# The exponential of a retrieval head's scores, taken by GpSimd as a power of e instead of by ScalarE

## The reference

```
q = (hb @ w_peer_q).reshape(PEER_BLOCK, PEER_HEADS, 2, PEER_HALF)
s = einsum('thpc,hpkc->thpk', q, sub_keys)          # 2 x 128 scores per head
s1, i1 = top_k(s[:, :, 0], 16); s2, i2 = top_k(s[:, :, 1], 16)
cand = s1[..., :, None] + s2[..., None, :]           # 256 candidates
top_s, top_c = top_k(cand, 16)
idx = e1 * 128 + e2                                  # from i1, i2, top_c
g = softmax(top_s)                                   # over the 16
a = einsum('td,tkd->tk', hb, expert_u[idx])
out = einsum('tk,tkd->td', g * gelu(a), expert_v[idx])
```

## Time and profile before

| | before |
|---|---|
| median of 3 runs | 2178.06 us |
| profiled execution, time | 2179.98 us |
| profiled execution, span | 2178.1 us |
| busy: PE, DVE, ACT, POOL | 1620.5, 1409.0, 846.7, 799.1 us |
| moved by DMA | 745.14 MB, mean 342 GB/s |
| gathers of expert rows (line 1113) | 544, median 11.5 us from issue to landing |

### The profile page before, as it was taken

The page is one execution under the profiler, slowest core; times in us unless marked ns, Lnnn a source line. Parts: engine busy times, 40 slices in busy tenths (PEclk is TensorE's granted clock), DMA queues, the critical chain, the costliest instruction groups (busy, mean ns, idle before and its releaser), DMA issues.

```text
span 2178.1 us, 33399 instructions
## 1 busy us (share of the span) xinstructions
PE 1620.5 (74%) x11692; PEld 743.6 (34%) x11692; DVE 1409.0 (65%) x3339; ACT 846.7 (39%) x2418; POOL 799.1 (37%) x713
## 2 busy tenths in 40 slices
PE   7989999898998987778788989986544445444343
PEld 3555655354444443434443433332100001100000
DVE  2577766124558687877777666446776776776774
ACT  2122333102554434545456652334333333333332
POOL 1254200001323254443443333334455555455553
PEclk9999999999999998988899999998655555655555
DMA  5333466837999898899999999999999999999998
GB/s 189 143 114 114 171 213 239 308 136 266 390 417 368 343 374 359 334 383 362 372 373 408 381 391 407 399 407 398 421 421 418 421 410 407 415 418 416 421 411 347
DMA packets 125794, 745.14 MB, mean 342 GB/s; under 512 B 15892, under 2 KB 39052, under 8 KB 47916
## 3 DMA queue, kind: packets, MB, share of 16 engines
q0 software_dynamic: 78336, 570.46, 64.7%
q1 hardware_dynamic: 47292, 172.55, 21.2%
HBM read 727.36 MB, written 16.44 MB: 342 GB/s over the span
## 4 chain that ended last, share of the span: by engine, by line
PE 35%; DMA 29%; DVE 22%; issue 7%; ACT 5%; POOL 2%; SPq 0%; DVEq 0%; ACTq 0%; POOLq 0%
DMA ring<-in_expert_uv,pick 27%; PE z L1181 20%; DVE ring L1961 8%; PE acc L1353 4%; PE z L1187 2%; PE o L1216 1%; POOL ring L1113 1%; PE s L1206 1%; DVE ti L1844 1%; DVE ti L1847 1%; DVE tmp L2032 1%; DVE nm L2058 1%; PE t L1407 1%; ACT fold L1526 1%; PE o L1269 1%
## 5 line engine op out<-in xcount | busy, mean ns | idle before, releaser
L1113 POOL DMA_INDIRECT ring<-in_expert_uv,pick x544 | 667.8, 1227 | 866.4 <-PE acc L1353 792.9
L1961 DVE CUSTOM_DVE_ANT_0 ring<-ring,rep 128x1024 f32<-128x1024 f32 x544 | 664.4, 1226 | 371.4 <-DMA ring<-in_expert_uv,pick 337.1
L1353 PE MATMUL acc<-ring,fold 128*32 128x256 f32 x4352 | 454.4, 509 | 410.0 <-ACT fold L1526 409.2
L1181 PE MATMUL z<-wts,hT 128*128 128x384 f32 (+1 forms) x1408 | 607.2, 569 | 5.2 <-ACT hT L1572 2.6
L1523 ACT ACTIVATE gel<-dots 128x1 f32<-128x1 f32 x544 | 109.6, 201 | 763.0 <-DVE dots L1961 762.3
L1353 PEld LDWEIGHTS acc<-ring,fold 128*32 128x32 f32 x4352 | 107.4, 125 | 726.7 <-ACT fold L1526 650.8
L1181 PEld LDWEIGHTS z<-wts,hT 128*128 128x128 f32 x1408 | 260.0, 199 | 256.3 <-issue 191.6
L1181 PE MATMUL z<-wts,yT 128*128 128x512 f32 x384 | 189.0, 628 | 11.9 <-ACT yT L1722 7.6
L1526 ACT ACTIVATE fold<-by_pick,gel 128x32 f32<-128x32 f32 x544 | 174.8, 321 | 18.0
L1519 ACT ACTIVATE by_pick<-cst,pick 128x32 f32<-128x32 f32 x544 | 167.2, 307 | 0.0
L1836 DVE SCALAR_TENSOR_TENSOR yT<-uT,vec,yT 128x256 f32<-128x256 f32 x240 | 107.8, 500 | 2.3
(11 more groups left out here) (256 smaller groups left out, 1686.7 us busy)
## 6 DMA issues: line engine op xcount, KB each, us to landing
wts<-in_w_qkv SPq DMA_DIRECT2D x24, 1536.0 KB, 7.7
wts<-in_w_glu SPq DMA_DIRECT2D x8, 2048.0 KB, 12.2
wts<-in_w_gate SPq DMA_DIRECT2D x8, 2048.0 KB, 12.4
wts<-in_w_wq SPq DMA_DIRECT2D x8, 2048.0 KB, 11.1
ring<-in_k_cache SPq DMA_DIRECT2D x16, 768.0 KB, 7.3
ring<-in_v_cache SPq DMA_DIRECT2D x16, 768.0 KB, 8.0
ring<-in_expert_uv,pick POOLq DMA_INDIRECT x544, 11.5
wts<-in_w_cp SPq DMA_DIRECT2D x4, 2048.0 KB, 11.1
```

Of the source, the lines that this page charges most:

```text
L1113: eng.indirect_dma_start(ring[:, i % RING, :], None, a["expert_uv"], bass.IndirectOffsetOnAxis(picks(i, 0).bitcast(U32), 0)).then_inc(row_ ...
L1181: mm = eng.matmul(bank[:, 0:w], of[:, k, :], rows[:, k, :], start=(k == 0), stop=(k == depth - 1))
L1353: mm = eng.matmul(acc[b][SUB * c:SUB * (c + 1), col:col + 256], fold[:, i % 4, :], ring[:, i % RING, D + 256 * c:D + 256 * (c + 1)], start ...
L1961: eng.tensor_tensor_reduce(u, u, rep[:, j, :], 1.0, 0.0, ALU.mult, ALU.add, dots[:, i % 4:i % 4 + 1]).then_inc(dot_ready, 1)
```

## The change

`head_exp` moves from ScalarE to GpSimd. There it adds `nmx` to `cv` and raises e to the result, from a constant tile `base_e` of 16 columns. It comes right behind the gather of step at+8 (part 3 of a head belongs to step at+3, and the code looks up `PARTS` at i - 5); item 0 is done at the start of tick START - 1. The row sum, which ScalarE gave along with the exponential, is now an instruction of VectorE in `experts`, behind the wait for `ex_ready` and ahead of the reciprocal.

```diff
+        base_e = sb("base_e", [P, TOPK])
...
 (GpSimd)
+            def head_exp(q):
+                eng.wait_ge(top_ready, q + 1)
+                link(eng.tensor_scalar(ex[:, :], cv[:, :], nmx[:, :], None, ALU.add))
+                eng.tensor_tensor(ex[:, :], base_e[:, :], ex[:, :], ALU.pow).then_inc(ex_ready, 1)
...
                     eng.indirect_dma_start(ring[:, i % RING, :], None, a["expert_uv"], ...).then_inc(row_in[i % RING], 16)
+                    for q, p in PARTS.get(i - 5, ()):
+                        if p == 3:
+                            head_exp(q)
...
+            link(eng.memset(base_e[:, :], float(np.e)))
...
             for n, tick in enumerate(TICKS):
+                if n == START - 1:
+                    head_exp(0)
                 if n >= START:
                     steps_upto(MARK[n - 1] + RING)
...
 (ScalarE)
-            def head_exp(q):
-                m = P
-                eng.wait_ge(top_ready, q + 1)
-                eng.activation(ex[0:m, :], cv[0:m, :], ACT.Exp, bias=nmx[0:m, :], accum_out=exs[0:m, 0:1]).then_inc(ex_ready, 1)
...
-                    for q, p in PARTS.get(i, ()):
-                        if p == 4:
-                            head_exp(q)
...
-                if n == START - 3:
-                    head_exp(0)
...
 (VectorE, experts)
                 eng.wait_ge(ex_ready, q + 1)
+                link(eng.tensor_reduce(exs[0:m, 0:1], ex[0:m, :], AX, ALU.add))
                 link(eng.reciprocal(exs[0:m, 1:2], exs[0:m, 0:1]))
```

## The result

The changed kernel takes 2188.34 us, the median of 8 runs (2186.22 to 2191.14), beside 2178.2 us before. The ratio is 1.0045, 95% interval 1.003 to 1.006: slower by 10 us. The forecast was 2180 us and no measurable difference, the range 2166 to 2198. What happened is by its mechanism the first rival, the gathers' queue running short (2194 us, chance 0.28), at a smaller price than it named. Of all executions reported in this document only two lie far off the rest, 2793.58 and 3858.56 us, both of e10_no_exponential, and its ratio leaves them out.

The account below looks back on a forecast made before the run. Expert-row transfers were taken to set the pace after 1492 us, a mixed chain before. Terms -4 (ScalarE), +1 and +5 (GpSimd, earlier and later stretch), 0 (VectorE) sum to +2 us on 2178.06: 2180 us, range 2166 to 2198.

Parts of the forecast that it names:

- the first rival: Later stretch: in each of 16 heads the late gather meets a nearly empty queue; 1.0 x 16, 2194 us, chance 0.28.
- ScalarE's part: Exponentials and table loads leaving ScalarE: 4 us off before 1492 us; 0 after, at most 1.0 us per head regained.
- The power's length, the addition's wait and the new gap: GpSimd, later stretch: power 2.9 us, addition held until the dot's end, gap near 7 us between gather issues.
- So it fits by 0.7 us, and at+10 by about as much.: Later stretch: the first delayed gather still lands 0.7 us before its dot, the next with about that margin.
- The size: Later-stretch cost of GpSimd's late gathers: 0.3 us per head, 5 us on; bounds 16 off to 16 on.
- a power of twice the length: GpSimd, later stretch: at twice 2.9 us the row would be 2.2 us late each time, 35 us in all.
- The earlier stretch on GpSimd: Before 1492 us: the same gather lateness but less gather time on the chain; 1 us on, bounds 0 and 17.
- The decision point of the rival: Later stretch: the queue runs short from a power of 3.6 us, or a short-queue landing over 6.2 us.
- Its sum at 0: VectorE's new sum of 16 columns: 0.2 us each, hidden by later row waits, worth 0; uncovered 7 us.
- The wait at the reciprocal: VectorE waiting for GpSimd's power: it ends 3 us early in later heads; first head 0, at most 1 us.
- The rule of the Trainium skill: GpSimd and VectorE locking shared ports: a dot waits for the power's end; as a rival 2190 us, chance 0.05.
- Marks that I named: Right: later heads 40.7 to 41.0 us apart, DMA share 0.99. Wrong: the 1492 us mark moving over 5 us.

Follow-up runs that it names:

- e10_no_exponential: Changed kernel without GpSimd's addition and power: no engine takes an exponential, the tile is set to one once and VectorE sums it; 2170.0 us.
- e1: Kernel before, ScalarE keeping the exponential but losing its row sum, which VectorE takes as its own instruction; 2177.0 us.
- e5: Changed kernel with the power left out: GpSimd's addition alone writes the tile and releases VectorE; 2174.0 us.
- e6_power_twice: Changed kernel with GpSimd's power taken twice, the first into a spare tile; 2256.0 us.
- e8_two_later: Changed kernel with GpSimd's exponential placed two gathers later than the change has it; 2209.2 us.
- e9_split_place: Changed kernel with GpSimd's exponential at the change's place in the earlier stretch and one gather later for the 16 later-stretch heads; 2174.3 us.

## Why the prediction was right in its range and wrong in its largest term

By medians, the path from before to after is: VectorE's sum -1 (e1; not distinguishable from 0), ScalarE's exponentials gone -7 (e10 against e1), the addition and its waits +4 (e5 against e10), the power +14 (changed against e5). Together +10. The single terms carry some 3 to 4 us of uncertainty each. The power's +14 and ScalarE's -7 are clear of it, the addition's +4 is not. The forecast was -4 + 1 + 5 + 0 = +2: slower by less than can be told from nothing.

- **ScalarE's part.** Forecast -4 in the earlier stretch and 0 in the later; measured -7 in all, of which 3.2 in the later by the spacing, leaving about 4. The 0 was too low: the spacing could give back up to 1.0 us a head by the forecast's own bound, and it gave 0.2.
- **The power's length, the addition's wait and the new gap.** Forecast 2.9 us, until the dot's end, and "a gap near 7 us"; measured 2.97 and 7.06. Right.
- **"So it fits by 0.7 us, and at+10 by about as much."** This is the step that failed, in its second half. At+9 fits in the head shown (it waits 0.23 us; two of the 16 heads wait over 1 us). At+10 does not: it was issued at 1952.84 and its dot began at 1961.54, 8.7 us later. The prediction gave it the same margin as at+9, that is, a row one pace of 2.48 us behind that of at+9. The two dots stand 4.06 us apart here and 3.27 on average, where they stood 2.55 apart before. The step checked whether one row would land in time. What counts is whether the DMA ever has nothing to move, and it has: between 8.0 and some 10 us behind the issue of at+8 it runs thin, as the rows of at+9 begin to flow only at 8.75. Why VectorE meets that hole at the second row and not the first is not settled.
- **The size.** I put 0.3 us per later head on it, net of nothing regained, and 5 us in all. Net of ScalarE's gain the spacing rose by 0.67, 10.7 us; the power alone takes 0.85 a head. The bound of 1.0 held it. By the estimated knee of 6.2 us a power of some 2.1 us would have cost nothing. The prediction's own figure for a power of twice the length, 35 us in all, was low as well: e6_power_twice is 77 us over the kernel before, 58 of them in the later stretch (44.32 - 40.70 = 3.62 a head, where the figure has 2.2).
- **The earlier stretch on GpSimd.** Forecast +1. Of the power's +14 and the addition's +4 the spacings place 13.6 and 1.1 in the later stretch, which leaves some 4 for the earlier one, not clear of the noise.
- **The decision point of the rival** was a power of 3.6 us or a landing over 6.2 us from a short queue. The second was about met at at+9 (6.0 us from issue to dot in the head shown, 6.3 on average) and clearly at at+10 (8.2 on average). Such a margin of 0.7 us, against a landing taken from the least of one window, deserved the larger chance. That the time still came out inside the range is owed to its width: it reached past this rival.
- **VectorE.** Its sum at 0: right, e1_sum_only. The wait at the reciprocal: 4.8 us in 2 heads, within the 1 us and its bound. The power did not hold VectorE back: the dot of at+5 starts at 1949.98, 1.66 us into the power, and it stands 3.19 us behind its predecessor where it was 3.16. In all 16 later heads it starts 0.5 to 1.3 us ahead of the power's end. The rule of the Trainium skill, "SBUF — State Buffer" (SBUF: two separate sides), in which the instruction that comes second waits for the whole of the first, would have had it wait. The trace does not agree with that half of the rule.
- **Marks that I named:** the heads stand 41.37 us apart, outside the 40.7 to 41.0 that I named for being right, so this sign told of the failure; the DMA share of the later stretch (1.00) did not. The 1492 us mark was of no use, since identical programs differ there by over 6 us.

## What to carry to other kernels

Where an engine issues the transfers that set the pace, work put on it has a free allowance, the backlog in the queue. Beyond it, the work cost its full length at each occurrence here (slope 0.97 between gaps of 7.06 and 10.09 us). Measure the allowance as a gap between issues: from an issue to the moment at which the DMA would run dry, less the time from an issue to its first rows (8.0 - 1.7 us here). Whether the next row lands in time is not the test. Here the same 2.97 us of work cost 14 us behind one gather and next to nothing behind the next, because there it did not first have to wait 2.3 us for its input and for a dot.

A wait has two ends: one place later filled the queue and starved the consumer in the other stage. Choose the place by stage: e9_split_place did, and was 4 us faster than the one place that suits the later stretch.

## What the runs showed of the hardware

- GpSimd's power of 16 columns takes 2.93 to 2.94 us when nothing holds it up; with 0.56 for 1 column and 1.35 for 6 it is a straight line, 0.16 us a column.
- GpSimd's addition of 16 columns lasts 0.34 us alone, 0.62 beside two-input VectorE work and 1.37 beside a dot. A power that starts before the dot does is hardly lengthened (2.93 to 3.06 us in the changed kernel). A power that starts while a dot runs can be: 3.85 us at 1285.45 in the changed kernel, up to 4.02 in e8_two_later. In no later head of the changed kernel does the dot of at+5, which starts inside the power, wait for the power's end.
- When the queue had run out, the rate took some microseconds to come back although the share did not show it: 12 to 14 us behind the issue of at+8 it is 355 GB/s at a share of 0.99 in the changed kernel (403 at 0.99 before), as the single 8 KB transfers take 362 ns there, 320 before, and 314 at the full rate. Why is open.
- Removing 63 table loads and 34 activations, over 90 us of an engine that is busy 39% of the time, was worth 7 us (e10_no_exponential against e1_sum_only), by the spacing nearly half of it in a stretch whose DMA share was 0.99 already.
